# Last attention of a two-layer block: scores and value products as three split products each

## The reference

```python
s = jnp.einsum('bqhgd,bkhd->bhgqk', q.reshape(b, tq, hkv, g, d), k).astype(jnp.float32) * d ** -0.5
p = jax.nn.softmax(s, axis=-1)
o = jnp.einsum('bhgqk,bkhd->bqhgd', p.astype(v.dtype), v)
```

## Time and profile before

| | |
|---|---|
| median of 3 runs | 2608.44 us (2606.38 to 2612.1) |
| the profiled execution's own time | 2603.68 us |
| its span | 2601.9 us |
| mean granted TensorE clock | 0.955 |
| busy in the whole span | PE 2377.1 (91%), PEld 1927.4 (74%), DVE 1222.1 (47%), POOL 1065.0 (41%), ACT 794.8 (31%) |
| the attention stage | first matmul at 2062.45, last GpSimd subtraction ends at 2172.38, next stage's first matmul at 2172.71 |

### The profile page before, as it was taken

The page is one execution under the profiler, slowest core; times in us unless marked ns, Lnnn a source line. Parts: engine busy times, 40 slices in busy tenths (PEclk is TensorE's granted clock), DMA queues, the critical chain, the costliest instruction groups (busy, mean ns, idle before and its releaser), DMA issues. The chain is left out here.

```text
span 2601.9 us, 35012 instructions
## 1 busy us (share of the span) xinstructions
PE 2377.1 (91%) x14323; PEld 1927.4 (74%) x14323; DVE 1222.1 (47%) x1930; ACT 794.8 (31%) x1301; POOL 1065.0 (41%) x728
## 2 busy tenths in 40 slices
PE   6987688999997989967889999999989999899998
PEld 5866466777775779855678888888877688688887
DVE  4517627856564670467426242332427752423422
ACT  4232424433335422334332121111124363322221
POOL 2325224655553322324235343343425124555553
PEclk8998897999998999979999999999989999899999
DMA  8470122544442112100113224333311101223231
GB/s 267 154 234 1 59 65 95 177 134 154 151 148 75 33 49 65 33 1 1 33 49 98 79 89 141 104 124 114 97 57 49 49 1 53 69 90 97 97 97 49
DMA packets 224701, 229.95 MB, mean 88 GB/s; under 512 B 7375, under 2 KB 221219, under 8 KB 224547
## 3 DMA queue, kind: packets, MB, share of 16 engines
q1 hardware_dynamic: 224211, 227.66, 27.2%
q10 hardware_dynamic: 336, 0.11, 0.0%
HBM read 225.65 MB, written 2.10 MB: 88 GB/s over the span
## 5 line engine op out<-in xcount | busy, mean ns | idle before, releaser
L1266 POOL TENSOR_TENSOR w_lo<-ring,w_hi 128x1024 fp32r<-128x1024 f32 x128 | 311.8, 2436 | 430.6 <-ACT w_hi L1261 430.6
L2073 DVE SCALAR_TENSOR_TENSOR xT<-ps,mods,xT 128x512 f32<-128x512 f32 (+1 forms) x160 | 108.5, 683 | 541.0 <-PE ps L1327 500.6
L1261 ACT ACTIVATE w_hi<-ring 128x1024 fp32r<-128x1024 f32 x128 | 135.7, 1060 | 737.9 <-PE ps L1327 701.8
L1325 PE MATMUL ps<-hidden_hi,w_hi 128*128 128x512 f32 (+1 forms) x768 | 273.9, 357 | 5.5 <-POOL hidden_lo L2436 5.5
L1326 PE MATMUL ps<-hidden_lo,w_hi 128*128 128x512 f32 (+1 forms) x768 | 272.1, 354 | 0.0
L1327 PE MATMUL ps<-hidden_hi,w_lo 128*128 128x512 f32 (+1 forms) x768 | 271.6, 354 | 0.0
L2359 DVE SCALAR_TENSOR_TENSOR ffn_sums<-ps,cols,ffn_sums 128x441 f32<-128x441 f32 (+2 forms) x352 | 215.0, 686 | 105.5 <-ACT ffn_sums L2280 105.5
L1325 PE MATMUL ps<-h_hi,w_hi 128*128 128x512 f32 (+1 forms) x720 | 256.3, 356 | 6.7 <-POOL w_lo L1266 3.0
L1326 PE MATMUL ps<-h_lo,w_hi 128*128 128x512 f32 (+1 forms) x720 | 255.0, 354 | 0.0
L1327 PE MATMUL ps<-h_hi,w_lo 128*128 128x512 f32 (+1 forms) x720 | 254.6, 354 | 0.0
L2426 DVE TENSOR_TENSOR squares<-squares 128x512 f32<-128x512 f32 (+1 forms) x72 | 145.1, 2015 | 217.1 <-ACT squares L2412 217.1
(11 more groups left out here) (438 smaller groups left out, 5257.3 us busy)
## 6 DMA issues: line engine op xcount, KB each, us to landing
ring<-in_mlp_w SPq DMA_DIRECT2D x64, 1024.0 KB, 5.3
ring<-in_ada_w SPq DMA_DIRECT2D x48, 1024.0 KB, 5.3
ring<-in_w_ada SPq DMA_DIRECT2D x24, 1024.0 KB, 9.6
ring<-in_ffn_w_up SPq DMA_DIRECT2D x22, 1024.0 KB, 7.1
ring<-in_ab_w_in SPq DMA_DIRECT2D x11, 1024.0 KB, 5.2
ring<-in_ffn_w_down SPq DMA_DIRECT2D x12, 768.0 KB, 5.9
ring<-in_w_in SPq DMA_DIRECT2D x8, 1024.0 KB, 7.7
ring<-in_c_w_in SPq DMA_DIRECT2D x6, 1024.0 KB, 5.0
```

Source lines behind the costliest of these rows:

```text
L1261: act.activation(w_hi[m][:, 0:x["kt"], :], ring[:, x["n"] % NS, 0:x["kt"], m * P:(m + 1) * P], ACT.Copy).then_inc(SW["w_hi"].sem, 1)
L1266: pool.tensor_tensor(w_lo[m][:, 0:x["kt"], :], ring[:, x["n"] % NS, 0:x["kt"], m * P:(m + 1) * P], w_hi[m][:, 0:x["kt"], :].bitcast(F32), ...
L1325: pe.matmul(o, w_hi[m][:, k, :], h, start=(k == 0), stop=False)
L2073: return nc.vector.scalar_tensor_tensor(x, bank, column_of(gates, t * 2 + 2 * gate + r), x, ALU.mult, ALU.add)
```

## The change

`attention` is replaced by `split_attention`:

- The queries, keys and values are split into high and low parts. ScalarE makes a high part (`part_high`, line 2709), GpSimd the low part (line 2592), eleven pairs of instructions in all: key head 0, query head 1 and value head 0 at the start of the stage, query head h (2 to 7) after the copy of job 4h - 5, value head 1 after job 4 and key head 1 after job 5. A low part is written over its source.
- `scores(j)` of heads 1 to 7 is three fp32r matmuls for each of the two pieces (lines 2614 to 2616). Those of head 0 stay float32 (line 2612).
- ScalarE's `take(j)` (line 2698) writes the rounded `p_hi`, and VectorE has a new step, `low(j)` (line 2673): `p_lo` = transposed PSUM minus `p_hi`, 128 x 768. `turn(j)` (line 2625) waits for `low(j - 1)` as well.
- `values(p)` (lines 2636 to 2638) is made once for a pair p of jobs, that is for 256 queries: eighteen fp32r matmuls of 256 columns, after `turn(j)` of every even j from 2, for jobs j - 2 and j - 1. `give(p)` (line 2703) and the GpSimd split are for 256 columns too.
- The weights of the next projection lie elsewhere in memory. Other stages are as they were.

The diff, cut to its core:

```diff
-        def attention(jobs, scale, bufs, made):
...
+        def split_attention(qc, kc, vc, out_t, sc, stat, scale, space, made):
+
+            n_jobs, n_pairs = 8 * NLAT, 4 * NLAT
...
+            p_hi, p_lo = parts("p_hi", [P, 2, NCH, 2 * P]), parts("p_lo", [P, 2, NCH, 2 * P])
+            k_hi, k0_lo = parts("k_hi", [P, 2, TOK]), parts("k0_lo", [P, TOK])
+            v_hi, q_hi = parts("v_hi", [P, NCH, SLAB]), parts("q_hi", [P, 2, LAT])
+            q_lo = rounded("q_lo", big_at, [P, 8, LAT])
+            k_lo = rounded("k_lo", big_at + 4 * 8 * LAT, [P, 2, TOK])
+            v_lo = rounded("v_lo", big_at + 4 * (8 * LAT + 2 * TOK), [P, NCH, SLAB])
...
+            ops = [("k", 0), ("q", 1), ("v", 0), ("q", 2), ("v", 1), ("k", 1)] + [("q", h) for h in range(3, 8)]
+            when = {("k", 0): -1, ("q", 1): -1, ("v", 0): -1, ("v", 1): 4, ("k", 1): 5}
+            when.update({("q", h): 4 * h - 5 for h in range(2, 8)})
...
                 @block.gpsimd
                 def _(pool):
-                    for j in range(n_jobs):
-                        h, n = divmod(j, NLAT)
-                        wait(pool, "pv_out", j + 1)
-                        made.split(pool, h, n * CH, CH)
-                        if j == n_jobs - 6:
-                            made.weights_low(pool)
+                    for i, (kind, index) in enumerate(ops):
+                        x, hi, lo = tiles[kind](index)
+                        wait(pool, "part_hi", i + 1)
+                        sig(pool.tensor_tensor(lo, x, hi.bitcast(F32), ALU.subtract), "part_lo")
...
+                            wait(pool, "pv_out", p + 1)
+                            made.split(pool, h, n * CH, 2 * CH)
+                            if p == n_pairs - 3:
+                                made.weights_low(pool)
...
-                        for k_ap, c0, mask in keys:
-                            dst = flat[:, (j % 2) * 1024 + c0:(j % 2) * 1024 + c0 + k_ap.shape[1]]
-                            ins = pe.matmul(dst, q, k_ap, start=True, stop=mask is None)
...
+                        if h and n == 0:
+                            wait(pe, "part_lo", max(ops.index(("q", h)), ops.index(("k", kv))) + 1)
+                        for c0, c1 in ((0, LAT), (LAT, TOK)):
+                            s_ps = flat[:, (j % 2) * 1024 + c0:(j % 2) * 1024 + c1]
+                            if h == 0:
+                                ins = pe.matmul(s_ps, qc[:, 0, q], kc[:, 0, c0:c1], start=True, stop=True)
+                            else:
+                                pe.matmul(s_ps, q_hi[:, h % 2, q], k_hi[:, kv, c0:c1], start=True, stop=False)
+                                pe.matmul(s_ps, q_hi[:, h % 2, q], keys_lo(kv)[:, c0:c1], start=False, stop=False)
+                                ins = pe.matmul(s_ps, q_lo[:, h, q], k_hi[:, kv, c0:c1], start=False, stop=True)
                         sig(ins, "qk")
 
                     def turn(j):
...
-                            wait(pe, "turned_out", j)
...
+                            wait(pe, "turned_a", j)
+                            wait(pe, "turned_v", j)
...
-                    def values(j):
-                        _, _, width, v, _, o = jobs[j]
-                        wait(pe, "turned_out", j + 1)
...
+                    def values(p):
+                        kv = p // (2 * NLAT)
+                        wait(pe, "turned_v", 2 * p + 2)
+                        wait(pe, "part_lo", ops.index(("v", kv)) + 1)
...
+                        for c in range(NCH):
+                            pe.matmul(o, v_hi[:, c, of_kv(kv)], p_hi[:, p % 2, c, :], start=(c == 0), stop=False)
+                            pe.matmul(o, v_hi[:, c, of_kv(kv)], p_lo[:, p % 2, c, :], start=False, stop=False)
+                            ins = pe.matmul(o, v_lo[:, c, of_kv(kv)], p_hi[:, p % 2, c, :],
+                                            start=False, stop=(c == NCH - 1))
                         sig(ins, "pv")
 
                     scores(0)
...
                         if j + 2 < n_jobs:
                             scores(j + 2)
                         turn(j)
-                        if j >= 1:
-                            values(j - 1)
-                    values(n_jobs - 1)
+                        if j >= 2 and j % 2 == 0:
+                            values(j // 2 - 1)
+                    values(n_pairs - 1)
...
+                    def low(j):
+                        wait(dve, "turned_a", j + 1)
+                        sig(dve.tensor_tensor(half(p_lo, j), turned_ps, half(p_hi, j).bitcast(F32), ALU.subtract), "turned_v")
 
                     top(0)
                     for j in range(n_jobs):
                         if j + 1 < n_jobs:
                             top(j + 1)
                         norm(j)
+                        if j >= 1:
+                            low(j - 1)
+                    low(n_jobs - 1)
...
+                        if j >= 4:
+                            wait(act, "pv", j // 2 - 1)
+                        sig(act.activation(half(p_hi, j), turned_ps, ACT.Copy), "turned_a")
+
+                    def give(p):
...
+                        sig(act.activation(out_t[:, h, n * CH:(n + 2) * CH], ps[:, 6 + p % 2, 0:2 * P], ACT.Copy), "pv_out")
+
+                    def part_high(step):
+                        for op in ops:
+                            if when[op] == step:
+                                x, hi, _ = tiles[op[0]](op[1])
+                                sig(act.activation(hi, x, ACT.Copy), "part_hi")
+
+                    part_high(-1)
                     expo(0)
                     for j in range(n_jobs):
                         if j + 1 < n_jobs:
                             expo(j + 1)
                         take(j)
-                        if j >= 1:
-                            give(j - 1)
+                        if j >= 2 and j % 2 == 0:
+                            give(j // 2 - 1)
+                        part_high(j)
                         if j == n_jobs - 7:
                             made.weights_high(act)
-                    give(n_jobs - 1)
+                    give(n_pairs - 1)
...
-                      [big_at + 4 * (24576 - (4 - i) * KT * P) for i in range(4)])
-        attention(jobs, 128.0 ** -0.5, bufs, c_made)
+                      [big_at + 4 * tabs_at] + [big_at + 4 * (24576 - (3 - i) * KT * P) for i in range(3)])
+        split_attention(qc, kc, vc, hT, bufs[0], bufs[1], 128.0 ** -0.5, big_at + 4 * c_lo_at, c_made)
```

More of the change, by code:

```diff
@@ L2567, in attention @@
             flat = ps[:, :, :].rearrange("p b n -> p (b n)")
-            n_jobs = len(jobs)
+            turned_ps = flat[:, 2048:2048 + TOK].rearrange("p (c n) -> p c n", c=NCH)
+            half = lambda buf, j: buf[:, (j // 2) % 2, :, (j % 2) * P:(j % 2 + 1) * P]
             with nc.Block() as block:
@@ L2600, in turn @@
+                            wait(pe, "turned_v", j)
+                        for c in range(NCH):
+                            ins = pe.transpose(turned_ps[:, c, :], sc[:, j % 2, c * P:(c + 1) * P], ident)
                         sig(ins, "turned")
-                    def values(j):
-                        _, _, width, v, _, o = jobs[j]
-                        wait(pe, "turned_out", j + 1)
[L2605 to L2610, removed]
+                    def values(p):
+                        kv = p // (2 * NLAT)
+                        wait(pe, "turned_v", 2 * p + 2)
+                        wait(pe, "part_lo", ops.index(("v", kv)) + 1)
+                        if p >= 2:
+                            wait(pe, "pv_out", p - 1)
+                        o = ps[:, 6 + p % 2, 0:2 * P]
+                        for c in range(NCH):
+                            pe.matmul(o, v_hi[:, c, of_kv(kv)], p_hi[:, p % 2, c, :], start=(c == 0), stop=False)
+                            pe.matmul(o, v_hi[:, c, of_kv(kv)], p_lo[:, p % 2, c, :], start=False, stop=False)
+                            ins = pe.matmul(o, v_lo[:, c, of_kv(kv)], p_hi[:, p % 2, c, :],
+                                            start=False, stop=(c == NCH - 1))
@@ L2625, in top @@
                     def top(j):
-                        _, _, width, _, sink, _ = jobs[j]
                         b = j % 2
@@ L2630, in top @@
                         wait(dve, "qk", j + 1)
-                        sig(dve.tensor_reduce(t, flat[:, b * 1024:b * 1024 + width], AX_X, ALU.max), "top")
+                        sig(dve.tensor_reduce(t, flat[:, b * 1024:b * 1024 + TOK], AX_X, ALU.max), "top")
                         wait(dve, "top", j + 1)
@@ L2634, in top @@
                             wait(dve, "exp", j - 1)
[L2635 to L2639, removed]
+                        sig(dve.tensor_scalar(m, t, -scale, None, ALU.mult), "max")
                     def norm(j):
-                        _, _, width, _, sink, _ = jobs[j]
                         b = j % 2
+                        den = stat[:, b, 1:2]
```

(8 more changed lines are left out.)

55 lines of the change are left out of this document (23 added, 32 removed).

## The result

The changed kernel takes 2624.67 us (median of 11 runs, 2617.15 to 2633.41); the kernel before takes 2607.28 on the same chips (11 runs, 2602.39 to 2614.14). The ratio is 1.0065, with a 95% interval of 1.0049 to 1.0082: slower by 17, at least 13 and at most 21. Forecast were +10.5 and a range from 2607 to 2629.

The account below looks back on a forecast made before the run. TensorE alone was taken to set the pace before; after, a closed chain of 7.02 a pair against 6.57. Middle +6.7, start +1.0 and end +2.8 made +10.5 on 2608.44, so 2618.9; range 2607 to 2629.

Parts of the forecast that it names:

- held-up `norm`: Rival: VectorE's `norm` is held up by GpSimd's new subtractions, +5.4 on top, 2624; chance 0.13.
- late high parts: ScalarE's later high parts, costed at nothing; without cover, 8 of them 5.5; the range kept a margin of 5.
- the clock: Rival: TensorE's clock falls because it stands idle more, +21 on top, 2640; chance 0.05.
- The chain: From one `low` to that two jobs later, through transposes, value products, scores, maximum and `norm`: 7.02 a pair against 6.57.
- The durations: Single instructions in the stage: `low` 0.96, fp32r matmuls 0.12 apart for 256 columns and 0.2265 for 512.
- The start: Start of the stage: `low(0)` now stands between `norm` and the transposes of job 1, +1.0.
- The middle: Transposes of job 4 to those of job 30: 84.6 before, 13 x 7.02 = 91.3 after, +6.7.
- `norm` beside GpSimd: VectorE's `norm` during GpSimd's subtractions, seven new ones in the middle: taken as 0, upper end 7 x 0.77 = 5.4.
- My rival with +5.4: Rival: GpSimd's new subtractions hold up VectorE's `norm`, +5.4 on top, 2624; chance 0.13.
- "Together 9.6. +2.8": End of the stage, from the last transposes to GpSimd's last subtraction: 9.6 after against 6.76 before, +2.8.
- "PEclk would stay at 1.00 from 2070 on": Expected in the profile after: TensorE's granted clock keeps 1.00 from 2070 on.
- the PEclk row that falls: Sign of being wrong: the profile's row for TensorE's granted clock falls.

Follow-up runs that it names:

- e8: Changed kernel with nine of a pair's eighteen value products behind each job's transposes and the result copy behind the odd job: stage 106.99, ratio 1.0001 against the kernel before.
- e9: e5 plus 23 TensorE products of 512 columns whose results nobody reads, in the waits at the stage's end: stage 120.94, ratio 1.0062 against the kernel before.
- e11: The changed kernel itself, unedited, with a second trace and more runs: stage 125.05, ratio 1.0055 against the kernel before.
- e5: Changed kernel with the next projection's first weights split earlier, at job 17 (ScalarE) and after pair 8 (GpSimd): stage 124.57, ratio 1.0069 against the kernel before.
- e4: Changed kernel without VectorE's `low`, the second value product reading the high part instead: stage 106.50, ratio 0.9999 against the kernel before.
- e7: Changed kernel with value products issued one job later and the result copy behind the odd job's copy: stage 117.81, ratio 1.0066, on repeat 117.91 and 1.0038.

## Why the prediction was right, and what was mis-sized

The direction and the mechanism were forecast. The size was not: +17.4 for +10.5, and 2624.67 lies above the 2614 to 2623 that the forecast itself covered. That it lies in the stated range is partly luck: the upper part of the range was there for a held-up `norm` (+5.4) and for late high parts (a margin of 5), while 4.4 of the 6.9 that came on top of the forecast were the clock's (2.7 at the end of the stage, 1.7 in the next projection), which the range left out.

**The chain** was right: 6.98 a pair where the sum gave 7.02, steps of 3.89 and 3.09, idle times of 1.40 and 1.22 where 1.3 and 1.4 were forecast, 21.2 in all for about 20. e8 shows that it is the order and not the work.

**The durations** held: `low` 0.952 for 0.96, matmuls 0.12 and 0.23 apart. The formula of the Trainium skill for isolated matmuls ("TensorE: Matmul & The Clock Gate", section "Back-to-back issue gap"), which gives 109 and 216 ns, was too low for these streams, as the rows had said.

**The start** was +0.7 up to the transposes of job 4, for +1.0.

**The middle** was 92.64 from the transposes of job 4 to those of job 30 (2080.24 to 2172.88) where I had 91.3. Thirteen pairs of 6.97 would be 90.6. The excess over that, 2.0, has a name, and I had costed it at nothing: `norm` beside GpSimd. Once it stood 1.14 instead of 0.62 beside the low part of value head 1:

```profile
2084.47 1.83 POOL L2592 TENSOR_TENSOR v_lo<-big,v_hi 128x768 fp32r<-128x768 f32 x1 [3.79 <-ACT v_hi L2709]
...
2085.58 1.14 DVE L2669 TENSOR_SCALAR big<-big,small 128x768 f32<-128x768 f32 x1
```

That pair took 7.49, 0.5 more than the others, and the pair with `weights_low` 1.46 more. Five other `norm`s stretched to 1.01 and cost nothing, since the pair around each stayed at 6.97 or 6.98: they belong to the job beside the chain. My rival with +5.4 had the right mechanism, but only 0.5 comes from one of the seven new subtractions that it counted. The other 1.46 comes from `weights_low`, which the kernel before had too: there `norm` took 1.39 beside it, and the transposes went on stepping by 3.29, because VectorE had room. In the chain the same collision costs its full length. By the Trainium skill ("SBUF — State Buffer", section "SBUF: two separate sides") VectorE needs the lock in a two-port mode or with two sources in SBUF; `low` has only one of its two sources there, and the trace agrees: all 32 `low`s took 0.944 to 0.958, whatever GpSimd did.

**The end is the step that failed.** "Together 9.6. +2.8" counts up to the end of GpSimd's last subtraction. Up to there it measured 12.4, against 6.76 before: +5.6. From there to the next projection is 0.63, against 0.33 before, and I had no term for that; together 13.03 against 7.09, +5.9. The sum was nearly right at full clock: e9, which keeps the clock, takes 10.31 to the next projection, which is the 9.6, that gap of 0.6 and 0.1 more. What failed is "PEclk would stay at 1.00 from 2070 on", and with it one of my own signs of being wrong came true, the PEclk row that falls, though only in the last 12 us of the stage. I had tested the clock against the middle, where TensorE is busy four fifths of the time, and found rightly that it holds there. The end has less work and longer waits, and I never asked it there. The two groups of value products took 3.7 and 3.5 instead of 2.16 each.

The terms: +0.7, +8.1 and +5.9 make 14.7. The next projection adds 1.7 (a clock of 0.66 over 5 us). That is 16.4, and the medians say 17.4; the rest is inside the interval. The stage terms and the clock come from one trace, which e11 repeats (125.05, the clock down at the end and in the next projection).

## What to carry to other kernels

When two in-order queues wait for each other, lay the loop out from one event to the same event one period later and add it up: that sum is the price, even if no engine is full, and splitting one block of work in halves can break it. A change that makes the busiest engine lighter may pay by halves (here the scores) and lose by the rest; time the parts apart. And ask the clock question at the thin places, the last two or three jobs before a barrier, not of the average.

## What I had not expected of the hardware

- TensorE's clock fell to half (steps of 0.21 for 256 columns instead of 0.12) in the last jobs of the change, behind an idle time of 3.72, and in e5 behind one of 2.27; in e4 it kept 1.00 behind one of 2.76, and in e7 behind 1.99, 1.89 and 2.31. Nor does the busy time of the 5 us just ahead of the first fall tell them apart (the first line is the change, the second e5), since e4 and e7 had stretches with less than e5 and no fall (third and fourth line). What the difference is stays open here.

```profile
2168.74:2173.74 5.00, 1.28 (x12) 1.08 (x11) 4.89 (x7) 1.71 (x4) 5.00 (x3) 1.00 0.00 0
2176.86:2181.86 5.00, 2.73 (x22) 2.40 (x21) 3.49 (x8) 2.96 (x6) 1.13 (x2) 1.00 0.00 0
2160.70:2165.70 5.00, 2.24 (x18) 1.88 (x16) 3.31 (x5) 2.96 (x6) 3.90 (x4) 1.00 0.00 0
2174.75:2179.75 5.00, 2.42 (x18) 2.21 (x18) 0.96 (x1) 1.47 (x3) 3.08 (x4) 1.00 0.00 0
```

- Work that nobody needs can shorten a stage: 23 products of 512 columns, 5.9 in all, saved 3.0 (e9 against e5).
- The granted clock in the stage's first 10 us lay between 0.71 and 0.85 from one execution to another. In the one with 0.71 (e5) the transposes of job 4 came 20.1 after the start of the stage; in the three others with the same instructions up to there (the change, e9, e11) it was 0.83 to 0.85, and they came after 19.3 to 19.5.
